# Norms in four pieces with the modulation mostly on VectorE, and the moves that go with it, in a two-layer backbone step

## What is computed

```python
for l in range(2):
    mix = concat(A, B, C) @ w_out[l]      # attention, gated DeltaNet scan, HGRN2 scan of p = h @ w_in[l]
    x = layer_norm(alpha * x + g1 * mix, ln_g[l, 0], ln_b[l, 0])
    h = x * (1 + scale2) + shift2
    f = swiglu(h) if l == 0 else moe(h)   # moe: top 2 of 8 experts
    x = layer_norm(alpha * x + g2 * f, ln_g[l, 1], ln_b[l, 1])

def layer_norm(x, g, b):
    mu = mean(x); var = mean(square(x - mu))
    return (x - mu) * rsqrt(var + eps) * g + b
```

## Time and profile before

| | us |
|---|---|
| median of 3 runs | 2576.73 |
| lowest and highest | 2572.4, 2581.18 |
| the profiled execution, its own time | 2566.51 |
| its span, first to last instruction | 2564.7 |

### The profile page before, as it was taken

One profiled execution on the slowest core, in us unless ns is written; L12 is line 12 of the kernel. 1 busy time (PEld: TensorE's weight loads), 2 busy tenths in 40 slices (PEclk: granted clock), 3 DMA queues, 4 the chain that ended last, 5 costly groups with the idle time before them and its releaser, 6 DMA issues.

```text
span 2564.7 us, 59573 instructions
## 1 busy us (share of the span) xinstructions
PE 2161.9 (84%) x25584; PEld 1325.7 (52%) x25584; DVE 1433.6 (56%) x1757; ACT 1294.5 (50%) x1711; POOL 749.2 (29%) x570
## 2 busy tenths in 40 slices
PE   4998986777879999998799777877947999999990
PEld 2665655654455555554557556644533444444440
DVE  2165734557433221214419656376247999999976
ACT  4433642344553332423533663355286778877762
POOL 1322113432322433423222124332212333333331
PEclk8999986977989999999899889687978999999995
DMA  9222892020031313213021000020175668891023
GB/s 280 78 83 87 286 325 91 5 54 3 21 99 50 98 50 98 82 65 86 28 68 36 1 4 5 4 54 11 28 253 195 226 222 304 308 347 50 34 99 131
DMA packets 214970, 278.54 MB, mean 109 GB/s; under 512 B 28129, under 2 KB 188493, under 8 KB 214607
## 3 DMA queue, kind: packets, MB, share of 16 engines
q1 hardware_dynamic: 203776, 243.60, 29.5%
q0 software_dynamic: 8576, 30.41, 3.2%
q10 hardware_dynamic: 2383, 1.11, 0.2%
HBM read 368.15 MB, written 29.11 MB: 155 GB/s over the span
## 4 chain that ended last, share of the span: by engine, by line
PE 52%; issue 16%; DVE 12%; ACT 8%; POOL 7%; DMA 4%; SPq 1%; POOLq 0%; ACTq 0%; DVEq 0%
PE ps L2207 50%; POOL mix L947 5%; DVE arena L1614 3%; DVE mix L1614 2%; DMA wbuf<-in_w_mod 2%; DVE mix L1622 1%; PE ps L2418 1%; ACT arena L1119 1%; ACT mix L1404 1%; DVE yg L1614 1%; POOL mix L950 1%; DMA const<-in_w_mod 1%; PE ps L2923 1%; DVE mix L1742 1%; SPq L631 1%
## 5 line engine op out<-in xcount | busy, mean ns | idle before, releaser
L2207 PE MATMUL ps<-hT,mix 128*128 128x512 f16 (+2 forms) x2784 | 380.4, 300 | 37.3 <-DVE hT L1614 27.7
L2207 PE MATMUL ps<-w,xgT 128*128 128x512 f16 x1632 | 365.8, 381 | 1.2 <-ACT xgT L1500 1.2
L2108 DVE SCALAR_TENSOR_TENSOR w<-wst,w 128x2048 f16<-128x2048 f32 x136 | 309.7, 2318 | 26.7 <-ACT w L1486 26.7
L2207 PEld LDWEIGHTS ps<-hT,mix 128*128 128x128 f16 x2784 | 220.1, 99 | 195.9 <-issue 47.5
L980 POOL TENSOR_TENSOR a<-aval,a 128x256 f16<-128x256 f32 x68 | 158.4, 2330 | 378.9 <-ACT a L1529 378.9
L1486 ACT ACTIVATE w<-wst 128x2048 f16<-128x2048 f32 x136 | 251.4, 1898 | 0.0
L2207 PEld LDWEIGHTS ps<-w,xgT 128*128 128x128 f16 x1632 | 157.5, 98 | 180.2 <-issue 3.5
L2207 PE MATMUL ps<-mix 128*128 128x512 f16 (+5 forms) x1856 | 212.5, 298 | 21.5 <-POOL mix L950 8.8
L2207 PE MATMUL ps<-hT,arena 128*128 128x128 f16 (+1 forms) x1440 | 199.6, 300 | 0.2 <-DVE const L1614 0.2
L2207 PE MATMUL ps<-w2m,aT 128*128 128x512 f16 x816 | 188.9, 382 | 2.6 <-DVE aT L2140 2.6
L2207 PEld LDWEIGHTS ps<-mix 128*128 128x128 f16 (+3 forms) x1856 | 126.1, 130 | 99.1 <-POOL mix L950 12.4
(11 more groups left out here) (359 smaller groups left out, 3543.7 us busy)
## 6 DMA issues: line engine op xcount, KB each, us to landing
wst<-in_moe_w SPq DMA_DIRECT2D x204, 1024.0 KB
wbuf<-in_w_mod SPq DMA_DIRECT2D x40, 1024.0 KB
wbuf<-in_ffn_w SPq DMA_DIRECT2D x33, 1024.0 KB
wbuf<-in_w_in SPq DMA_DIRECT2D x20, 1024.0 KB
xs_rows<-in_table SPq DMA_DIRECT2D x17, 512.0 KB, 14.3
xg<-xs_rows POOLq DMA_DIRECT2D x17, 512.0 KB, 4.4
ys_rows<-yb POOLq DMA_DIRECT2D x17, 512.0 KB, 2.9
wbuf<-in_w_out SPq DMA_DIRECT2D x32, 256.0 KB
```

The lines of the kernel that those rows point to most:

```text
L2108: v_.scalar_tensor_tensor(out=q[1], in0=staged(s, p), scalar=WS, in1=q[0], op0=ALU.mult, op1=ALU.subtract).then_inc(sg["m_lo13"], 1)
L2207: return mm_(o, w, x, start=first, stop=last, skip_group_check=True)
```

## The change

- `PIECES` becomes four: 128, 192, 192 and 128 tokens. DVE applies scale and shift in pieces 0, 1 and 3, and ACT in piece 2 alone. The orders of the operations on both engines change with it.
- Layer 0's third piece of the first FFN weights is split earlier on ACT (`weights(0, True)`).
- In layer 1 the logits are made as each piece of `h` is there, and `route` starts after the last. ACT no longer applies the norm's weight and bias to `xT`. Instead DVE makes eight diagonal matrices (`diag`) ahead of the output projection, and `to_rows_x` multiplies each block of `xT` by its diagonal and adds the bias row (`brow`, loaded by POOL) by a one-row product. One `xk` job stands before `rank` and four behind it. The PSUM slots of these jobs are named by hand.
- The end of the FFN: `yacc` goes into `xT` before the last slab, and the last slab's outputs go from PSUM straight into `xT`. Four of the eight averages stand between output tiles 6 and 7.
- The pieces of `w_mod` of layer 1 are streamed in another order, so that `gate_rows` stands in unit 17 instead of after unit 19. DVE waits for `near_in` only before `first_tiles(0)`, and POOL before `masked(0)`. SP waits for `near_in` before the blank writes. Slots of `grow0` and `G0` change.
- At the start `first_mods(2)` goes behind the load of `qa0`. ACT splits `qa0` between modulation rows 5 and 6, and `qa1` inside `upper_h` after its sixth tile.

The diff, cut to its core:

```diff
 def mod_piece(i):
-    return (0, i + 8) if i < 16 else (1, i - 16)
+    if i < 16:
+        return 0, i + 8
+    return 1, i - 16 + (4 if 32 <= i < 36 else -4 if i >= 36 else 0)
...
-                j += ["g2r"] * (x == len(units) - 1)
+                j += ["g2r"] * (x == 17)
...
-        j += ["2:grow0", "2:rf0", "2:G0", "2:KQ0"]
+        j += ["3:grow0", "2:rf0", "0:G0", "2:KQ0"]
...
         if l % 2:
-            j += ["router", "ht0", "ht1", "ht2", "xk0", "xk1", "rank", "ht3", "ht4", "xk2", "xk3", "xk4"]
+            j += ["2:router", "1:ht0", "0:ht1", "3:ht2", "1:ht3", "0:ht4", "3:xk0", "2:rank", "1:xk1", "0:xk2", "3:xk3", "2:xk4"]
...
-        PIECES = ((0, slice(0, 256)), (0, slice(256, LAT)), (1, slice(LAT, NT)))
+        PIECES = ((0, slice(0, 128)), (0, slice(128, 320)), (0, slice(320, LAT)), (1, slice(LAT, NT)))
...
-            first_mods(2)
...
+                        sp.wait_ge(sg["near_in"], 16)
...
+                    if name == "0.qa0":
+                        first_mods(2)
...
+                pool.wait_ge(sg["near_in"], 16 * (l + 1))
+                pool.wait_ge(sg["g2_out"], 32)
...
+                        if l:
+                            pool.dma_start(brow, ln_b[1, 0:1]).then_inc(sg["row_b"], 16)
...
+                    if k == 5:
+                        upper(l, "qa1")
...
...
-            for i in range(4, 8):
-                mod_row(0, i)
+            mod_row(0, 4)
+            mod_row(0, 5)
+            upper(0, "qa0")
+            mod_row(0, 6)
+            mod_row(0, 7)
...
-                    upper(l, "qa0")
-                    upper(l, "qa1")
...
+                    if l == 0 and x == 17:
+                        copy(g2row[0:2, :], L.full("0.g2r")[0:2, :], "0.g2r")
+                        for i in range(2):
+                            act.dma_start(g2_rows[i:i + 1, :], g2row[i:i + 1, :]).then_inc(sg["g2_out"], 16)
...
-                    act.wait_ge(sg["oa_lo"], UNITS)
-                    copy(g2row[0:2, :], L.full("0.g2r")[0:2, :], "0.g2r")
-                    for i in range(2):
-                        act.dma_start(g2_rows[i:i + 1, :], g2row[i:i + 1, :]).then_inc(sg["g2_out"], 16)
+                    L.full("1.mt4")
...
-                    def modulated(v):
+                    def upper_of(v):
...
-                        for k in range(KT):
+                        for k in range(KT) if v == 2 else ():
...
-                    for v, (_, c) in enumerate(PIECES):
-                        L.done(J(f"mean{i}")) if v == 2 else L.need("centred")
+                    def square(v):
+                        c = PIECES[v][1]
+                        L.done(J(f"mean{i}")) if v == 3 else L.need("centred")
                         L.do(a.activation(z[:, :, c], xT[:, :, c], ACT.Square), "sq_ready")
+                    square(0)
+                    square(1)
                     root(0)
+                    square(2)
                     root(1)
-                    modulated(0)
+                    upper_of(0)
+                    square(3)
                     root(2)
-                    modulated(1)
-                    modulated(2)
+                    root(3)
+                    for v in range(1, 4):
+                        upper_of(v)
...
+                    L.do(a.activation(id16[:, :], ident, ACT.Copy), "id_ready")
                     norm(1)
-                    for k in range(KT):
-                        L.do(a.activation(xT[:, k, :], xT[:, k, :], ACT.Identity, scale=lnr[:, 2, 0, k:k + 1],
-                                          bias=lnr[:, 2, 1, k:k + 1]), "x_ready" if k == KT - 1 else None)
...
-                def weights(i):
+                def weights(i, first=False):
...
-                        act.wait_ge(ps_full[bank], i * 3 + (base[bank] + k))
+                        if first:
+                            L.full(J("wo3"))
+                        else:
+                            act.wait_ge(ps_full[bank], i * 3 + (base[bank] + k))
...
-                weights(0)
+                weights(0, True)
...
-                    tt(xT[:, :, c], xT[:, :, c], wide(r, c), ALU.mult, to="scaled")
+                    tt(xT[:, :, c], xT[:, :, c], wide(r, c), ALU.mult, to="scaled" if v == 2 else None)
+                def modulated(v):
+                    g, c = PIECES[v]
+                    for k in range(KT):
+                        ts(z[:, k, c], xT[:, k, c], lnm[n][:, 0, k, g:g + 1], ALU.mult, lnm[n][:, 1, k, g:g + 1], ALU.add,
+                           to="scaled" if k == KT - 1 else None)
...
...
-                    tt(xT[:, :, c], xT[:, :, c], wide(s, c), ALU.subtract, to="centred", job=j if v == 2 else None)
+                    tt(xT[:, :, c], xT[:, :, c], wide(s, c), ALU.subtract, to="centred", job=j if v == 3 else None)
                 scale(0)
+                modulated(0)
...
+                modulated(1)
                 scale(2)
+                scale(3)
                 lower(1)
+                modulated(3)
                 lower(2)
+                lower(3)
...
-                if l:
-                    dve.wait_ge(sg["g2_out"], 32)
...
-                dve.wait_ge(sg["near_in"], 16 * (l + 1))
...
+                dve.wait_ge(sg["near_in"], 16 * (l + 1))
...
+                for k in range(KT) if l else ():
+                    ts(diag[k], ident, lnr[:, 2, 0, k:k + 1], ALU.mult)
...
+                for m in range(KT):
+                    for g, a0, a1 in groups:
+                        stt(xT[:, m, a0:a1], yacc[:, m, a0:a1], modT[:, l, 40 + m, g:g + 1], xT[:, m, a0:a1], ALU.mult, ALU.add)
...
-                    summed(end, m)
-                    dve.wait_ge(ps_free[b], end * 3 + base[b] + 2 + m // 4)
+                    turn = end * 3 + base[b] + 1 + m // 4
+                    dve.wait_ge(ps_full[b], turn + 1)
                     for g, a0, a1 in groups:
-                        stt(xT[:, m, a0:a1], yacc[:, m, a0:a1], modT[:, l, 40 + m, g:g + 1], xT[:, m, a0:a1], ALU.mult, ALU.add,
-                            to="z_ready" if g else None)
+                        ins = v_.scalar_tensor_tensor(out=xT[:, m, a0:a1], in0=ps[:, b, a0:a1], scalar=modT[:, l, 40 + m, g:g + 1],
+                                                      in1=xT[:, m, a0:a1], op0=ALU.mult, op1=ALU.add)
+                    ins.then_inc(ps_free[b], 1)
+                    dve.wait_ge(ps_free[b], turn + 1)
...
-                    L.done(J(f"wo{k}")) if i == 1 else L.need("z_ready")
+                    if i == 1:
+                        L.done(J(f"wo{k}"))
+                    else:
+                        pe.wait_ge(ps_free[k % 4], 3 * (SLABS[l] - 1) + base[k % 4] + 2 + k // 4)
...
-                def slab(i, first=False):
+                def slab(i, first=False, last=False):
...
                         down(m, 1).then_inc(ps_full[b], 1)
+                        if last and m == 6:
+                            open_(J("mean2"))
+                            for k in range(4):
+                                average(2, k)
...
-                with pe.Fori(1, SLABS[0]) as s:
+                with pe.Fori(1, SLABS[0] - 1) as s:
                     slab(s)
-                open_(J("mean2"))
-                for k in range(KT):
+                slab(SLABS[0] - 1, last=True)
+                for k in range(4, KT):
                     ins = average(2, k)
...
             def to_rows_x(t):
...
-                for k in range(KT):
-                    ins = tr_(s[:, k * P:(k + 1) * P], xT[:, k, t * P:(t + 1) * P], ident)
+                for h in range(2):
+                    mm(s[:, h * 512:h * 512 + 512], ident[0:1, 0:1].broadcast_to([1, P]), brow[:, h * 512:h * 512 + 512],
+                       True, False)
+                    for k in range(4 * h, 4 * h + 4):
+                        ins = mm(s[:, k * P:(k + 1) * P], xT[:, k, t * P:(t + 1) * P], diag[k], False, k % 4 == 3)
...
             L.need("wr_ready")
-            s = open_("1.router")
-            for t in range(TT):
+            L.need("id_ready")
+            logits = open_("1.router")
+            def routed(t):
...
-                        ins = mm(s[:, t * NE:(t + 1) * NE], h2[a_][:, k, t * P:(t + 1) * P], wr2[b_][:, k],
+                        ins = mm(logits[:, t * NE:(t + 1) * NE], h2[a_][:, k, t * P:(t + 1) * P], wr2[b_][:, k],
                                  k + a_ + b_ == 0, (k, a_) == (KT - 1, 1))
-            close(ins, "1.router")
-            L.need("id_ready")
+                return ins
...
             def to_rows(t):
...
-            for t in range(3):
+            for t in range(2):
+                L.need("h_ready")
+                routed(t)
                 to_rows(t)
-            L.need("x_ready")
+            L.need("h_ready")
+            routed(2)
+            routed(3)
+            to_rows(2)
+            L.need("h_ready")
+            close(routed(4), "1.router")
+            to_rows(3)
+            to_rows(4)
+            pe.wait_ge(sg["row_b"], 16)
```

(5 more changed lines are left out.)

32 lines of the change are left out of this document (14 added, 18 removed).

## The result

The changed kernel takes 2555.3 us (median of 5 runs, 2548.5 to 2558.8) against 2572.7 of the kernel before beside it (2571.1 to 2581.2). The ratio is 0.992, 95% interval 0.990 to 0.994. So the change brings 17 us, where the prediction had 46 and a range that ends at 2550. The profiled execution has a span of 2546.7 us where the kernel before had 2564.7, 18.0 less.

The account below looks back on a forecast made before the run. The prediction took TensorE's matmul work (52% of the chain, 16% more issue) as the bound and looked for its waits. Terms 12.2 + 1.5 + 8.3 + 10.6 + 15.4 - 1.8 = 46.2 us gave 2530.5 from 2576.7, range 2514 to 2550.

Parts of the forecast that it names:

- Routing: Layer 1, last norm to first expert matmul: earlier `h`, ranks and scatter, and faster transfers gain 15.4 us (1 to 17).
- rival A: Layer 1's product tiles run at the low clock, about 7.5 us each; routing gains 1, total 2544.9; chance 0.13.
- The cover: Layer 1: 15 us of products behind `rank` hide beside the scatter and its landing, some 11 us to spare.
- another 4.2: Layer 1's scatter: DVE's weight splits start when nine of ten transfers are issued, gaining 4.2 us more.
- they now wait for it: Layer 0's scan entry: blank writes that delayed the mask load (10.7 us) now wait for that load.
- The start: First products of `h`: first piece 3 us earlier, last tile at 71.3 instead of 67.5; TensorE loses 1.8 us.
- TensorE, which is behind anyway: Start of the kernel: TensorE lags its inputs, so the later last tile nets a 1.8 us loss (3 lost, 3 gained).
- The end of attention: Layer 0: DVE's first scan operation comes at 384.8 instead of 396.6, no longer ended by `nearb`; gains 11.8 us.
- D: Layer 0, end of attention: early gate rows do nothing, costing their full 3.5 us twice; term 8, total 2535; chance 0.06.
- Norms and the end of the FFN: Layer 0's two norms gain 10.6 us (0 to 14) through smaller pieces; the FFN's end gains 8.3 without the stall.
- B: Norms: small DVE operations cost 0.5 us fixed, not 0.27; layer 0's norms gain nothing, routing 7 less; 2548; chance 0.08.
- C: Both scans run at a clock of 0.6, not about 0.8; 80 us slower, 2611; decides from 54 us; chance 0.03.

Follow-up runs that it names:

- combination 2: Changed kernel with the kernel before's start, blank writes moved to layer 1, and the shift `ln_b` added on TensorE with 128 input rows: 2530.4 us, ratio 0.982.
- old start: Changed kernel with the start of the kernel before (both modulation loads ahead of `w_in`, `qa0` and `qa1` split after the eight modulation rows): 2547.6 us, ratio 0.989.

## Why the prediction was wrong

**Routing, 15.4 forecast, -0.2 measured.** Everything ahead of the ranks came out: the first scatter 43.0 us after the first centring (42.9 forecast), ten transfers in 12.4 us (13). The step that failed is the choice of the clock for the four tiles behind the ranks. I priced a tile at 3.8 us from averages that have 128 input rows, and set rival A, with 7.5 us a tile and a term of 1, to 0.13, because "from t = 27 on TensorE has no gap". There was no gap, and the clock was low. Rival A's price of a tile (7.5, measured 8.0), its end of the tiles (72, measured 68.7 after the centring) and its consequence, that the expert rows wait for them, were right. Its reason, bursts and idle stretches, was not, and its ranks 4 us later didn't come, because the tile ahead of them ran at the full clock. The cover was said to be what can go, with 11 us to spare at the full clock. At 8.0 us a tile instead of 3.8 it was used up. A second step of this term failed too: "another 4.2" for the faster transfers, with "the tail" behind them unchanged. The transfers were faster, but the landing took it back (20.3 and 20.2 us from the first scatter to the load). So with 128 input rows the term is 11.6 (81.3 less 69.7) or 12.0 (combination 2), and not 15.4.

**The scan of layer 0, +9.9 where nothing was forecast.** The step was "they now wait for it": I followed the blank writes out of the mask load's way and didn't ask what they would run into. They cost 4.6 us there by the runs. The rest is within the scatter of the scan, which one trace of before couldn't show; 338.6 and 336.9 in its two layers looked like a constant, and the first turned out to be the shortest of thirteen.

**The start, 1.8 forecast, 3.2 measured** (DVE's first scan operation, 389.7 against 386.5 with the old start, 3.0 by the means; 6.0 at the end of the first products, against the kernel before). The last tile was forecast for 71.3; tile 6 came at 71.9 and the last at 72.7. The first product came 1.5 us earlier (55.02 against 56.56) and not 3. What failed was "TensorE, which is behind anyway". By 67.6 it had done the 72 matmuls that were to be had, stood still for 4.39 us and then ran 120 in 19.14 us, where they take 16.4 at the full clock (192 such take 26.24 in the FFN, at a clock of 1.00). A part of the 6.0 is absorbed in attention.

**The end of attention, 11.8 forecast.** With the old start DVE begins its scan at 386.5, 10.1 us earlier than before (384.8 forecast). The last piece then comes 1.7 us later than before (2.6 forecast), and from it to DVE's start it is 9.9 us where I had 7.3; the last turn alone takes 3.54 us in the changed kernel, not 2. So D doesn't hold: the early gate rows don't cost their full price. The 3.1 us that the table misses up to DVE's start are about what the six kernels with the same code up to there differ by (387.9 to 391.1).

**Norms and the end of the FFN, 18.9 forecast, 19.5 measured.** This is right by its parts too: from the first centring of norm 1 to the last slab's 66 matmuls it is 5.5 us less (5.3 forecast), from there to norm 2 8.1 less (8.3). In norm 1 `h` was there at 13.4, 21.6, 26.4 and 27.9 us (14, 22, 27, 28). B doesn't hold: eight operations of 128 and 192 columns take 3.03 and 3.30 us (3.0 and 3.3), by the line that was laid through the forms of the earlier trace rows. The Trainium skill's page "VectorE: DVE Perf Modes", section "The TRN2 errata", gives 58 cycles plus half the columns, an estimate of 0.13 us at 128 columns. Here it is contradicted too: one takes 0.35 us.

**C** doesn't hold: the longest scan of any kernel, 351.5 us, is 13 us over the one before, where C decides from 54.

## To carry over

When a transfer is moved out of one wait, look at what runs while it runs in its new place; here long rows of very small matmuls lost 4.6 us beside 9 MB of writes of which they read nothing. Judge TensorE's clock by the shape of what it does and not by the absence of gaps: here products that use one input row cost twice their price and that of their neighbours, and the same result with 128 rows was 2.3 times as fast. Where a wait ends with the landing of a transfer, a faster issue alone may bring nothing. And where a term is hidden behind cover, price it at the low clock too before calling it free.

## What the hardware showed that was not expected

- Products with one input row between products with 128: granted clock 0.50 with TensorE busy 100% of the time, for 30 us. With 128 input rows in the same places it was 1.00 (8.0 against 3.5 us a tile). Seven traces with the one-row form show it.
- 17 transfers of 512 KB beside unrolled code of small matmuls: 4.6 us more over 38.4, of which 4.4 are in gaps that have only issue ahead of them.
- A scan of some 345 us takes between 204.9 and 215.9 us in its longest part, over thirteen traces whose code there is the same (the longest has the blank writes beside it, the next has 214.5), so a single trace can't price 5 us there.
- 16 operations of DVE from and to SBUF, with a split of POOL's of 4.12 us over them, took 13.75 us and not 9.2; pairs with an input in PSUM took 1.01 each under POOL's split at 1194.84.
